# Seven-product blocks whose weight sums are only additions, made in part by an accumulating transfer from GpSimd

## What is computed

```python
h = _rmsnorm(x, norm_g[l])
proj = h @ w_in[l]
...
g = jax.nn.sigmoid(gl.reshape(B, S, N_BRANCH, D_MODEL) + b_gate[l])
merged = g[:, :, 0] * ua + g[:, :, 1] * ub + g[:, :, 2] * um
x = x + (merged @ w_out[l]).astype(x.dtype)
```

## Time and profile before

| | us |
|---|---|
| median of 3 runs | 1158.67 (1158.09 to 1158.79) |
| the profiled execution | 1158.19 |
| its span, first to last instruction | 1156.4 |
| TensorE busy | 1149.4 |
| VectorE busy | 842.6 |
| ScalarE busy | 580.8 |
| GpSimd busy | 44.4 |

### The profile page before, as it was taken

One profiled execution on the slowest core, in us unless ns is written; L12 is line 12 of the kernel. 1 busy time (PEld: TensorE's weight loads), 2 busy tenths in 40 slices (PEclk: granted clock), 3 DMA queues, 4 the chain that ended last, 5 costly groups with the idle time before them and its releaser, 6 DMA issues.

```text
span 1156.4 us, 14201 instructions
## 1 busy us (share of the span) xinstructions
PE 1149.4 (99%) x5253; PEld 955.8 (83%) x5253; DVE 842.6 (73%) x1064; ACT 580.8 (50%) x715; POOL 44.4 (4%) x37
## 2 busy tenths in 40 slices
PE   8999999999999999999999999999999999999998
PEld 7788888888888888888888888888888888888887
DVE  6686588576567567567566666789769858988997
ACT  6565545445445545535444454545535544554643
POOL 1110000000010000000000000000000000000000
PEclk9999999999999999999999999999999999999999
DMA  9998789658577587677678786755865685485872
GB/s 335 316 287 297 259 269 330 216 189 288 194 237 268 196 272 250 214 256 234 244 240 264 246 262 204 229 171 174 291 209 182 238 262 166 162 291 182 271 243 104
DMA packets 147944, 276.00 MB, mean 239 GB/s; under 512 B 9709, under 2 KB 32933, under 8 KB 147888
## 3 DMA queue, kind: packets, MB, share of 16 engines
q1 hardware_dynamic: 135808, 258.31, 66.5%
q10 hardware_dynamic: 11600, 16.87, 4.9%
q0 software_dynamic: 480, 0.07, 0.0%
HBM read 251.34 MB, written 26.24 MB: 240 GB/s over the span
## 4 chain that ended last, share of the span: by engine, by line
PE 99%; DMA 0%; DVE 0%; issue 0%
PE acc L1721 26%; PE acc L1725 26%; PE acc L1729 26%; PE acc L1958 3%; PE acc L1954 3%; PE acc L1960 3%; PE side L1926 1%; PE side L1929 1%; PE side L1931 1%; PE acc L1929 1%; PE acc L1926 1%; PE acc L1931 1%; PE side L1958 1%; PE side L1960 1%; PE side L1954 1%; PE side L1760 1%
## 5 line engine op out<-in xcount | busy, mean ns | idle before, releaser
L1085 DVE TENSOR_TENSOR w_lo<-w_raw,w_hi 128x1024 fp32r<-128x1024 f32 x261 | 317.9, 1221 | 206.0 <-ACT w_hi L699 205.3
L699 ACT ACTIVATE w_hi<-w_raw 128x1024 fp32r<-128x1024 f32 x261 | 276.0, 1059 | 308.3 <-PE acc L1729 289.5
L1721 PE MATMUL acc<-w_hi,hT_hi 128*128 128x512 f32 x956 | 257.0, 391 | 0.0
L1725 PE MATMUL acc<-w_lo,hT_hi 128*128 128x512 f32 x956 | 255.6, 389 | 0.0
L1729 PE MATMUL acc<-w_hi,hT_lo 128*128 128x512 f32 x956 | 255.6, 389 | 0.0
L1725 PEld LDWEIGHTS acc<-w_lo,hT_hi 128*128 128x128 f32 x956 | 179.4, 188 | 37.5
L1729 PEld LDWEIGHTS acc<-w_hi,hT_lo 128*128 128x128 f32 x956 | 179.4, 188 | 37.4
L1721 PEld LDWEIGHTS acc<-w_hi,hT_hi 128*128 128x128 f32 x956 | 178.1, 188 | 36.9 <-issue 0.9
L1595 DVE TENSOR_TENSOR w_lo<-w_raw,w_hi 128x1024 fp32r<-128x1024 f32 x128 | 155.4, 1219 | 44.0 <-ACT w_hi L1013 43.7
L1013 ACT ACTIVATE w_hi<-w_raw 128x1024 fp32r<-128x1024 f32 x128 | 134.4, 1057 | 102.3 <-PE acc L1729 82.7
L1013 ACT ACTIVATE w_hi<-group 128x1024 fp32r<-128x1024 f32 x36 | 38.2, 1062 | 51.8 <-PE acc L1960 40.1
(11 more groups left out here) (274 smaller groups left out, 1275.4 us busy)
## 6 DMA issues: line engine op xcount, KB each, us to landing
w_raw<-in_w_in_dram SPq DMA_DIRECT2D x130, 1024.0 KB, 5.8
w_raw<-in_w_mem_kv_dram SPq DMA_DIRECT2D x16, 1024.0 KB, 6.4
w_raw<-in_w_in_dram SPq DMA_DIRECT2D x27, 512.0 KB, 4.9
w_raw<-in_w_proj_a_dram SPq DMA_DIRECT2D x12, 1024.0 KB, 7.1
w_raw<-in_w_proj_m_dram SPq DMA_DIRECT2D x8, 1024.0 KB, 8.0
w_raw<-in_w_proj_b_dram SPq DMA_DIRECT2D x8, 1024.0 KB, 5.2
w_raw<-in_w_out_dram SPq DMA_DIRECT2D x16, 512.0 KB, 5.0
w_raw<-in_w_out_dram SPq DMA_DIRECT2D x8, 1024.0 KB, 6.9
```

The lines of the kernel that those rows point to most:

```text
L699: act.activation(whi[:, ring(u0, s)], raw[:, slot, UK * (s % 2):UK * (s % 2) + UK], ACT.Copy)\
L1085: dve.tensor_tensor(wlo[:, ring(u0, s)], raw[:, (l0 + s // 2) % RING, UK * (s % 2):UK * (s % 2) + UK], whi[:, ring(u0, s)].bitcast(F32), A ...
L1721: pe.matmul(banks[t][:], x_pair[0][:, k + j, toks[t]], whi[:, at, j], start=first and j == 0, stop=False)
L1725: pe.matmul(banks[t][:], x_pair[0][:, k + j, toks[t]], wlo[:, at, j], start=False, stop=False)
```

## The change

The basis of the seven products is another one: the weights are only added. The four raw tiles of a block are two of depth k and two of k + 1 in the two chunks. Now tile (k, chunk 1) is loaded twice, into the two upper places of the slot, (k, chunk 0) and (k + 1, chunk 1) into the two lower ones, and (k + 1, chunk 0) into a buffer of its own, outside of the ring (`alone`, two halves that the blocks take in turn). Then GpSimd issues one transfer that adds the two lower tiles to the two upper ones (`add_weights`). VectorE makes two sums of 512 columns from the result. The unit q = 0 works on the tile outside, q = 1 on the two lower tiles, q = 2 on what the transfer made, q = 3 on VectorE's sums. Token sums and fold take the signs and places that belong to this basis; their number of operations stays.

```diff
-            if u[0] == "c" or u[2] < 2:
+            if u[0] == "c" or u[2] < 3:
                 ends[u[3]] = i
...
+            def alone_free(n):
+
+                if n == 1:
+                    sp.wait_ge(ts_lo, 2)
+                elif n < FIRST_OUT:
+                    sp.wait_ge(folded, 8 * (n - 1))
+                else:
+                    sp.wait_ge(m_out, 64 * (n - 1))
...
+                            j = k // 2
+                            if j == 0:
+                                alone_free(n)
+                            b12 = views[1][:, k:k + 1, 0:CW].to_broadcast([P, 2, CW])
+                            sp.dma_start(raw[:, slot, 2:], b12).then_inc(load_in[slot], 16)
+                            sp.dma_start(raw[:, slot, 0], views[0][:, k, 0:CW]).then_inc(pair_in[slot], 16)
+                            sp.dma_start(raw[:, slot, 1], views[1][:, k + 1, 0:CW]).then_inc(pair_in[slot], 16)
+                            sp.dma_start(areas(n)[0][:, j % 2], views[0][:, k + 1, 0:CW]).then_inc(pair_in[slot], 16)
...
+            def add_weights(n, j):
+
+                ld = block_load(n, j)
+                slot = ld % RING
+                pool.wait_ge(load_in[slot], 16 * (ld // RING + 1))
+                pool.wait_ge(pair_in[slot], pair_signals(n, ld))
+                pool.dma_start(raw[:, slot, 2:], raw[:, slot, 0:2], accum_op=ALU.add).then_inc(sums_in[slot], 16)
+
+            for n in range(1, FIRST_OUT + 2):
+                for j in range(PLANS[n].blocks):
+                    add_weights(n, j)
...
-                        act.activation(whi[:, at, 0], raw[:, slot, 0], ACT.Copy).then_inc(hi_done, 1)
+                        act.activation(whi[:, at, 0], alone[:, j % 2], ACT.Copy).then_inc(hi_done, 1)
                         return
                     if q == 2:
-                        act.wait_ge(t13_done, blocks_done(n, j))
+                        act.wait_ge(sums_in[slot], sums_landed(n, ld))
                     if q == 3:
-                        act.wait_ge(t4_done, blocks_done(n, j))
-                    source = (raw[:, slot, UK:], t13, t42)[q - 1]
+                        act.wait_ge(b_done, blocks_done(n, j))
+                    source = (raw[:, slot, 0:2], raw[:, slot, 2:], sums)[q - 1]
...
-                    dve.tensor_tensor(t13, r[:, 1::2], r[:, 0:2], ALU.subtract).then_inc(t13_done, 1)
...
-                    dve.tensor_tensor(t42[:, 1], r[:, 3], t13[:, 0], ALU.subtract).then_inc(t2_done, 1)
...
-                    dve.tensor_tensor(t42[:, 0], r[:, 2], t42[:, 1], ALU.subtract).then_inc(t4_done, 1)
...
+                dve.wait_ge(sums_in[ld % RING], sums_landed(n, ld))
+                dve.tensor_tensor(sums[:, 1], r[:, 2], r[:, 1], ALU.add).then_inc(b112_done, 1)
+                dve.wait_ge(pair_in[ld % RING], pair_signals(n, ld))
+                dve.wait_ge(b112_done, done)
+                dve.tensor_tensor(sums[:, 0], sums[:, 1], alone[:, j % 2], ALU.add).then_inc(b_done, 1)
...
-                    dve.tensor_tensor(fold[1], p5[:], fold[1], ALU.add).then_inc(folded, 1)
+                    dve.scalar_tensor_tensor(fold[1], fold[1], -1.0, p5[:], ALU.mult, ALU.subtract).then_inc(folded, 1)
...
+                    lo_pair(n, s)
                     weight_sums(n, s)
-                    lo_pair(n, s)
...
-                work = (((a11, p1),), ((a12, p2), (b4, p3)), ((b1, p5), (b3, p7)), ((a22, p4), (b2, p6)))[q]
+                work = (((a12, p2),), ((a11, p1), (b4, p3)), ((b3, p5), (b2, p7)), ((a22, p4), (b1, p6)))[q]
```

More of the change, by code:

```diff
@@ L158, in starts @@
         for i, (kind, at, q, ld) in enumerate(self.units):
[L159 removed]
+            for bank in (((2, 4), (3, 8))[at] if kind == "c" else ((2,), (1, 3), (5, 7), (4, 6))[q]):
                 first.setdefault(bank, i)
@@ L190, in block_load, with pair_signals, sums_landed @@
     return LOAD0[n] + PLANS[n].loads.index(("s", 0, 2 * j))
-def halved(n, ld):
+def pair_signals(n, ld):
+    every = [(LOAD0[m] + i, 3 if x[0] == "s" else 1) for m in range(1, n + 1) for i, x in enumerate(PLANS[m].loads)
+             if x[0] in "sb" and LOAD0[m] + i <= ld]
+    return 16 * sum(count for x, count in every if x % RING == ld % RING)
+def sums_landed(n, ld):
     every = [LOAD0[m] + i for m in range(1, n + 1) for i, x in enumerate(PLANS[m].loads)
-             if x[0] in "sb" and LOAD0[m] + i <= ld]
-    return sum(x % RING == ld % RING for x in every)
+             if x[0] == "s" and LOAD0[m] + i <= ld]
+    return 16 * sum(x % RING == ld % RING for x in every)
 def blocks_done(n, j):
@@ L998, in hi_pair @@
                 if s < plan.len and plan.loads[plan.units[s][3]][0] in "sb":
[L999 removed]
+                    act.wait_ge(pair_in[slot], pair_signals(n, ld))
                 if s < plan.len and plan.units[s][0] == "s":
[L1001 to L1002 removed]
+                    kind, j, q, _ = plan.units[s]
+                    alone, sums, fold = areas(n)
                     if q == 0:
[L1004 removed]
+                        act.activation(whi[:, at, 0], alone[:, j % 2], ACT.Copy).then_inc(hi_done, 1)
                         return
                     if q == 2:
[L1007 removed]
+                        act.wait_ge(sums_in[slot], sums_landed(n, ld))
                     if q == 3:
[L1009 to L1010 removed]
+                        act.wait_ge(b_done, blocks_done(n, j))
+                    source = (raw[:, slot, 0:2], raw[:, slot, 2:], sums)[q - 1]
                 else:
@@ new lines, in weight_sums @@
+                j = plan.at.index(s)
+                done = blocks_done(n, j)
+                alone, sums, fold = areas(n)
+                ld = block_load(n, j)
+                r = raw[:, ld % RING]
+                if j:
+                    dve.wait_ge(lo_done, u0 + plan.at[j - 1] + 4)
+                elif n < FIRST_OUT:
+                    dve.wait_ge(*((m_out, 64 * (n - 1)) if n > 1 else (oz_out, 64 * GROUPS)))
+                elif n == FIRST_OUT:
+                    dve.wait_ge(chunk_taken, 2 * CHUNK[NCH - 1] + 6)
+                else:
+                    dve.wait_ge(mixed, 4 * NCH)
@@ L1585, in lo_pair @@
                 if s < plan.len and plan.units[s][0] == "s":
-                    q = plan.units[s][2]
-                    t13, t42, fold = areas(n)
+                    kind, j, q, _ = plan.units[s]
+                    alone, sums, fold = areas(n)
                     if q == 0:
-                        dve.tensor_tensor(wlo[:, at, 0], r[:, 0], whi[:, at, 0].bitcast(F32), ALU.subtract)\
+                        dve.tensor_tensor(wlo[:, at, 0], alone[:, j % 2], whi[:, at, 0].bitcast(F32), ALU.subtract)\
                             .then_inc(lo_done, 1)
                         return
-                    source = (r[:, UK:], t13, t42)[q - 1]
+                    source = (r[:, 0:2], r[:, 2:], sums)[q - 1]
                 else:
```

51 lines of the change are left out of this document (14 added, 37 removed).

## The result

The changed kernel takes 1172.68 us as a median of five runs (1169.61 to 1177.37), against 1158.67 us before: slower, ratio 1.0128 with a 95% interval of 1.0100 to 1.0156. It also spreads more: 7.8 us from the fastest run to the slowest, where the kernel before had 0.9 us. The profiled execution is the slowest of the five, 1177.37 us; its span is 19.2 us longer than that of before. I explain those 19.2 us first, and use medians where kernels are compared.

A forecast was written before the change was run, and what follows sets the result against it. TensorE's matmul count was taken to bound the kernel, with VectorE off the path; output-pair stalls of 1.6 and 1.7 us less 0.4 us gave +2.9 us on the 1158.67 us median, 1161.6 us, range 1158.0 to 1171 us.

The forecast's parts named there:

- TensorE bounds the stages and VectorE's relief is worth under 1 us: Block stages: TensorE busy 385.08 of 385.10 us; work saved elsewhere gains at most 0.8 us.
- Loads, issues, basis, fold and the later release cost nothing by themselves: Block stages: four loads per block, 256 KB more (0.65 us) and later slot release (2.9 us) stall nothing by themselves.
- the predicted 1087.1 us: First output pair, third block: load landing forecast as 1077.56 + 8.9 + 0.65 us.
- The transfer takes 7.7 us, between 6.4 and 10.3 us: GpSimd's adding transfer of 512 KB, issue to landing: 5.1 + 2.6 us, bounds 6.4 and 10.3 us.
- The sum: Whole kernel: stalls of 1.6 and 1.7 us less 0.4 us gained, +2.9 us, giving 1161.6 us.
- Stops of 1.6 and 1.7 us in the output pairs: Third blocks of both output pairs: TensorE waits for a low part, 1.6 us near 1096 and 1.7 us near 1140.
- The gate stages stay whole: Gate stages: with a 7.7 us transfer TensorE does not wait there, 0 us.
- The limits there: Gate stages: room for the transfer before TensorE waits, 10.3 us at the third block and 9.6 us at the fourth.
- The prediction's own sign: Gate stages: if TensorE waits there too, the forecast is wrong and the transfer takes over 10 us.
- the 0.4 us of gain: Output pairs: gain from TensorE's wait for the last pair's first small unit, behind a removed VectorE difference, 0.4 us.
- The rival of a far slower transfer (13 us): Transfer of 13 us or more stalls gate stages and output pairs, +32 us, about 1190 us; chance 0.06.
- the one of sums in time: Block stages: VectorE's sums are back in time, not slower, 1158.3 to 1160.9 us, most likely 1158.6; chance 0.42.

## Why the prediction had the right place and the wrong size

- *TensorE bounds the stages and VectorE's relief is worth under 1 us.* Right: without the transfer 1158.39 us, TensorE busy 385.10 of 385.10 us.
- *Loads, issues, basis, fold and the later release cost nothing by themselves.* Right, by the same run and by the one in which VectorE adds. But they were not without effect on the chain. In the first output pair TensorE began the third block at 1100.87 instead of 1095.18 us, 5.7 us later than before, so the last piece of its load, issued at 1084.95, landed at 1084.95 + 8.5 - 5.7 = 1087.8 on the old time scale, against the predicted 1087.1 us; in the second pair the block began 12.3 us later, and the piece issued at 1132.91 landed at 1132.91 + 10.7 - 12.3 = 1131.3 against 1129.7 us. I had counted the 256 KB at the full rate and nothing for two more issues of SP in front of the last piece, nor for the load ahead, which was issued later and was still under way. A term mis-sized by 0.7 and 1.6 us in this execution, and by 2.0 us in the run in which VectorE adds: there the first pair's block began at the same time as before, and its load landed at 1089.1 us.
- *The transfer takes 7.7 us, between 6.4 and 10.3 us.* The third blocks had 8.8 and 7.9 us: inside the bounds, 1.1 and 0.2 us over the value. Its parts were wrong: the fixed part is about 1.9 us by the estimate above, not 5.1 us. That the tiny transfers of the earlier trace rows had spent the rest in the full queues of their stretch is likely and was not tried. The rest of the third blocks' times is 2.6 us for the adding and 3 to 4 us behind other loads. The sum also had no term between the load's landing and the transfer's issue; it took 0.7 and 0.6 us.
- *Stops of 1.6 and 1.7 us in the output pairs.* Place and instruction were right, the low part of unit 1 at the third blocks; the sizes were 4.4 and 4.8 us. The 2.8 us missing in the first pair are the load 0.7, the issue 0.7, the transfer 1.1 and VectorE's chain 0.2 us; the 3.1 us missing in the second are the load 1.6, the issue 0.6, the transfer 0.2 and VectorE's chain 0.5 us.
- *The gate stages stay whole.* Wrong in this execution: 2.4 and 0.8 us. The limits there were 10.3 and 9.6 us from a landing that I had put at the time of a quiet DMA; the fourth block's load was in flight beside the third one's transfer and took longer itself. The last piece of it took 7.0 to 8.0 us to land in the three gate stages, and 4.3 to 4.7 us in the two runs that have no transfer by GpSimd. So transfer and loads delay one another. The prediction's own sign, that TensorE waits in the gate stages only if the transfer takes over 10 us, was wrong with it: the waits came with transfers of 7.1 and 8.5 us. The page's group of the eighteen first sums has 29.3 us of idle time for the transfer, nearly all in the eight waits of the list above, of which only two are the output pairs' third blocks; so the room is used up in the gate stages too:

```profile
L1602 DVE TENSOR_TENSOR group<-w_raw 128x512 f32<-128x512 f32 x18 | 12.4, 688 | 29.3 <-DMA w_raw<-w_raw 29.3
```

- *The step that failed.* Two steps of the sum. It charged a stop with its own length only (the prediction's words are that what comes late to TensorE is added in full): the clock had no term. TensorE was granted half of its clock behind every stop of 2.4 us or more, and that added 1.7, 2.6 and 2.2 us in the profiled execution, 6.5 us where the sum had nothing. And it took room and chain too favourably, with loads, issue and transfer as above: 9.2 us of stops in the output pairs against 3.3 us, and 3.2 us in the gate stages against none. Stops make 9.1 us and the clock 6.5 us of the 16.3 us that the profiled execution lies above the sum; the 0.4 us of gain did not show either. That 9.2 us of stops and 4.8 us of clock in the output pairs give the median's 14 us is chance, since they were measured in the slowest run. The run at the median has a mean clock of 0.997, so the clock cost it at most about 3.5 us (0.003 of 1171 us), and its stops were not seen.
- *The chances.* Slower had 0.55 and came; the range ended at 1171 us, 1.7 us below the median. It was made from the ends of the transfer's time and did not hold the clock; without the clock's part the median might have lain inside it. The rival of a far slower transfer (13 us) did not come; the one of sums in time held for the first two blocks of all stages, and the later ones undid it. That rival's estimate of 3.2 us for the transfer fits a plain copy alone on the DMA; the addition took 4.5 us alone and up to 9.7 us beside loads.

What stays open: why the run time varies by 8 us. The traces give hints. The last piece of the load of the first output pair's third block took 8.4 to 10.8 us to land in the ten executions profiled after the change. The gate stages are the same instructions in the changed kernel and in three experiments (the stop filled, the loads held back, VectorE's addition in the output pairs), and the stops there were 3.2 us in all in the first and 1.1, 1.8 and 2.1 us in the others, with a fall of the clock only in the first. But of the changed kernel itself only the slowest execution's stops were seen, so this is an argument and no more. The release of the block's slot is not what makes the load of the third block late, as the issue times show; the 256 KB, the two more issues and the later load ahead were not tried apart.

## What to carry to other kernels

A step that is moved off an engine with idle time into a longer chain gives nothing when that engine was not the bound, and it takes the chain's room: reckon each block from load issue over landing and the transfer to the instruction that stands in order behind the wait, and do it for the block with the latest load, not the average one. In this case a transfer's time was its own bytes (about twice for an addition), a fixed part, and what was queued on the same engines at that moment; measure the last from rows of the same stretch. The link that gets faster or slower also moves the loads beside it, so reckon both. If TensorE stops for a few microseconds, add the stretch at the lower clock behind it.

## What the runs showed of the hardware that was not expected

- Adding 512 KB from SBUF to SBUF by GpSimd's transfer: 4.5 us alone, up to 9.7 us beside loads; copying them: 2.9 us alone. In the stretch of the first kind the DMA engines were as busy as beside full loads (1.03) and moved 199 GB/s, where loads moved 389 to 402 GB/s. GpSimd was held for 0.88 us by each adding issue, where copying ones took 0.53 us and its tiny ones 0.5 to 0.7 us.
- The last piece of a load took 4.3 to 4.7 us where no transfer by GpSimd was beside it, and 7.0 to 8.0 us beside an addition (fourth blocks of the gate stages).
- The granted clock stayed 1.00 behind stops of up to 2.0 us and was 0.50 behind stops of 2.4, 3.2, 4.4, 4.7, 4.8 and 4.8 us, for some 3 to 5.5 us; behind the 2.7 and 1.1 us that stood together in the run with later sums it was 0.50 for 6.5 us. With matmuls on a tile of zeros in the stop it stayed 1.00: one of the two operands was zero throughout, so that TensorE works was enough.
